# Selection masks in a sparse-attention block: expanded by matmuls with a 0/1 matrix, or read back from a stored copy with repeated rows

## The reference, cut to what matters

```
importance = einsum('bgsn,nm->bgsm', sum(p_cmp, axis=2), overlap)    # (B, G, S, 32)
sel_score  = where(forced & valid, 1e4, where(valid, importance, -1e4))
_, sel_idx = top_k(sel_score, 16)             # per query and group: 16 of 32 blocks of 64 keys
mask       = key_pos <= t                     # inside the chosen blocks
p          = masked_softmax(q @ K_chosen, mask);  out = p @ V_chosen
```

## Time and profile before

| what | value |
|---|---|
| times of the runs shown | 6959.97, 7552.63 (the median), 7947.71 us |
| profiled execution | 6946.9 us, its span 6945.3 us |
| cores in it | even 6864.7 to 6872.9 us, odd 6942.8 to 6945.4 us |
| PE busy | 6812.9 us (98%) |
| PE on the chain that ended last | 93% |
| DVE, ACT busy | 2238.7 us (32%), 1169.3 us (17%) |
| stage B of core 1 | from about 1394 to 2600 us, attention until about 2500 us |

### The profile page before, as it was taken

How to read it: one execution, slowest core, us unless ns; L and a number is a source line. 1 busy time by engine, 2 the same in 40 slices (tenths; PEclk the granted TensorE clock), 3 DMA queues, 4 the chain that set the end, 5 groups by cost and what they waited for, 6 DMA issues and landing times.

```text
span 6945.3 us, 98178 instructions; the slowest of 8 cores (6864.7 to 6945.4 us)
## 1 busy us (share of the span) xinstructions
PE 6812.9 (98%) x37468; PEld 3534.2 (51%) x37468; DVE 2238.7 (32%) x4038; ACT 1169.3 (17%) x2168; POOL 452.0 (7%) x727
## 2 busy tenths in 40 slices
PE   7999999989999999999999999999999999999997
PEld 4644454445555544466654444444444444444665
DVE  5418889544444513324430111111111111111134
ACT  4001110234444410013320000000000000000221
POOL 0000000000000000011100000000000000000110
PEclk9999999999999999999999999999999999999999
DMA  9645655778764355678854456775676766644798
GB/s 253 156 91 96 111 104 106 163 124 146 140 131 101 73 127 121 118 204 290 296 116 79 97 117 135 122 120 121 154 168 116 122 124 154 141 78 81 232 322 310
DMA packets 312533, 1017.19 MB, mean 146 GB/s; under 512 B 27360, under 2 KB 113248, under 8 KB 286720
## 3 DMA queue, kind: packets, MB, share of 16 engines
q0 software_dynamic: 160176, 707.98, 51.8%
q1 hardware_dynamic: 149440, 298.72, 13.1%
q10 hardware_dynamic: 2448, 4.13, 0.2%
HBM read 1381.75 MB, written 202.70 MB: 228 GB/s over the span
## 4 chain that ended last, share of the span: by engine, by line
PE 93%; DMA 3%; DVE 1%; issue 1%; SPq 1%; ACT 1%; DVEq 0%; ACTq 0%; POOLq 0%
PE bank L1403 54%; PE bank L352 28%; PE bank L1435 6%; PE bank L1143 2%; PE bank L1118 2%; DMA xr<-xc_t 1%; SPq L131 1%; DMA p_conv<-cstg 1%; PE bank L769 0%; DMA p_q<-sgb 0%; PE bank L1215 0%; DMA wslot<-w_dn_b 0%; DMA out<-yr 0%; DVE yr L1724 0%; DMA p_kv<-sgb 0%
## 5 line engine op out<-in xcount | busy, mean ns | idle before, releaser
L1403 PE MATMUL bank<-merged,wslot 128*128 128x496 bf16 (+2 forms) x11264 | 2119.4, 351 | 1.7 <-DVE merged L1444 1.7
L352 PE MATMUL bank<-uT,wslot 128*128 128x496 bf16 (+1 forms) x8768 | 1900.2, 375 | 0.0
L1403 PE MATMUL bank<-actq,wslot 128*128 128x496 bf16 (+2 forms) x9216 | 1718.2, 349 | 5.4 <-DMA wslot<-w_dn_b 4.1
L1403 PEld LDWEIGHTS bank<-merged,wslot 128*128 128x128 bf16 x11264 | 1102.1, 98 | 1018.3 <-issue 2.7
L352 PEld LDWEIGHTS bank<-uT,wslot 128*128 128x128 bf16 x8768 | 856.7, 98 | 952.5 <-issue 6.3
L1403 PEld LDWEIGHTS bank<-actq,wslot 128*128 128x128 bf16 x9216 | 901.3, 98 | 821.7 <-issue 8.0
L1595 DVE SCALAR_TENSOR_TENSOR rlE<-bank,acc 128x496 f32<-128x496 f32 (+2 forms) x262 | 173.5, 662 | 1489.0 <-PE bank L1403 1488.6
L1601 ACT ACTIVATE actq<-rlE 128x496 bf16<-128x496 f32 (+2 forms) x262 | 159.0, 607 | 2804.1 <-DVE rlE L1595 2804.1
L665 DVE SCALAR_TENSOR_TENSOR yb<-glu,cps,yb 128x992 f32<-128x992 f32 x480 | 600.0, 1250 | 43.2 <-DVE yb L665 1.8
L1121 ACT ACTIVATE emt<-bank 128x512 bf16<-128x512 f32 (+1 forms) x736 | 349.3, 529 | 367.3 <-PE bank L1118 268.0
L1650 DVE TENSOR_TENSOR ost<-bank,part 128x496 f32<-128x496 f32 x128 | 86.3, 674 | 770.3 <-PE bank L1403 770.3
(11 more groups left out here) (180 smaller groups left out, 3075.5 us busy)
## 6 DMA issues: line engine op xcount, KB each, us to landing
wslot<-w_in_t POOLq DMA_DIRECT2D x150, 1024.0 KB, 10.2
wslot<-w_up_t POOLq DMA_DIRECT2D x122, 1024.0 KB, 8.9
wslot<-w_out_b POOLq DMA_DIRECT2D x96, 1024.0 KB, 6.8
...
```

The source lines that it names most:

```text
L352: fns = [lambda kc=kc, bk=bk: nc.tensor.matmul(bk[:, 0:n], wt[:, kc * 128:(kc + 1) * 128], rhs[:, kc, lo:lo + n], start=(kc == 0), stop=(k ...
L1403: fns = [lambda kc=kc: nc.tensor.matmul(bk[:, 0:n], wt[:, kc * 128:(kc + 1) * 128], rhs[:, kc, lo:lo + n], start=(kc == 0), stop=(kc == KC ...
```

## The change

`expand` by matmuls and casts goes. The turned choice `selT` is stored in DRAM (`p_sel`, one 32 x 512 slice for each step), and the mask tiles are read back from it: for a group of 4 key tiles two loads, one into partitions 0 to 63 and one into 64 to 127, each repeating a row of 512 queries over 64 partitions. The steps of the choice move: `sel_transpose` from `wj0` + 11 to `wj0` + 5, the loads come at `wj0` + 6 and `wj0` + 7, the diagonal cuts at `sj0` - 4 to `sj0` - 1, `load_q` and `load_kv` from `wj0` + 8 to `wj0` + 12. `emats` and its clearing by DVE, and that of `selT`, go on the odd cores. Lines after the top of the file move by one or two: L1206 is L1204 afterwards, L1143 is L1141, L1118 is L1116, L1157 is L1155.

```diff
--- before.py
+++ after.py
@@ -186,6 +186,7 @@
     p_ga = dscr("p_ga", [32, 128, TMAX], BF16)
     p_gb = dscr("p_gb", [32, 128, TMAX], BF16)
     p_attn = dscr("p_attn", [16, 128, TMAX], BF16)
+    p_sel = dscr("p_sel", [8, 32, 512], BF16)
     p_conv = dscr("p_conv", [16, 128, TMAX], BF16)
     p_x1 = dscr("p_x1", [128, KC * TMAX])
     w_out_b = dscr("w_out_b", [32, 128, D], BF16)
@@ -931,14 +932,14 @@
             obf = Tile("obf", [128, 4, 512], BF16, Rw.end)
             ostg = Tile("ostg", [128, 2, 512], BF16, obf.end)
             imp = Tile("imp", [128, 4, 32], F32, ostg.end)
-            KE = 128 if h else 32
-            selT = Tile("selT", [KE, 512], BF16, imp.end)
+            selT = Tile("selT", [32, 512], BF16, imp.end)
             selm = Tile("selm", [128, 4, 32], BF16, selT.end)
             tk = Tile("tk", [128, 2, 32], F32, selm.end)
             mx = Tile("mx", [128, 16], F32, tk.end)
             sm = Tile("sm", [128, 12], F32, mx.end)
-            emats = Tile("emats", [KE, 2048], BF16, sm.end)
+            emats = Tile("emats", [32, 1024], BF16, sm.end)
             assert emats.end <= eb["lo"]
+            pselB = [Buf() for _ in range(8)]
             goff = gatesT_off - base
             selvs = Tile("selvs", [128, NT * 32], F32, goff + 2048)
             selbs = Tile("selbs", [128, NT * 32], F32, goff + 3072)
@@ -986,13 +987,10 @@
             VT = ((False, 0, 8), (False, 8, 4), (True, 0, 8), (True, 8, 8)) if h else ((False, 0, 8), (False, 8, 0), (True, 0, 8), (True, 8, 0))
             load_kv(0, ("vs",))
             if h:
-                K.op(dve, lambda: nc.vector.memset(emats[:], 0.0), w=[ematB])
-                K.op(dve, lambda: nc.vector.memset(selT[:], 0.0), w=[selTB])
-            K.dma(sp, emats[0:32, :], emat[:, :], w=[ematB])
-            if h:
                 K.dma(sp, selvs[:], selv[:, :], w=[selvB])
                 K.dma(sp, selbs[:], selb[:, :], w=[selbB])
             else:
+                K.dma(sp, emats[:], emat[:, 0:1024], w=[ematB])
                 K.dma(sp, tmk[:], tmsk[:, :, :], w=[tmkB])
                 K.dma(sp, tsl[:], tsel[:, :, :], w=[tslB])
                 K.dma(sp, wpd[:], wpad[:, :], w=[wpdB])
@@ -1206,18 +1204,19 @@
                 fns = [lambda t=t: nc.tensor.transpose(out=pst[0:32, t * 128:(t + 1) * 128], in_=selm[:, t, :], identity=idb[:])
                        for t in range(4)]
                 K.group(pe, fns, r=[selmB, constB], w=[bb])
-                K.op(act, lambda: nc.scalar.copy(out=selT[0:32, :], in_=pst[0:32, 0:512]), r=[bb], w=[selTB])
-
-            def expand(s, jt):
-                bk, bb = ring_bank("aux")
-                lo = max(0, jt * 128 - (1024 + (s % 2) * 512))
-                diag = jt * 128 >= 1024 + (s % 2) * 512
-                K.op(pe, lambda: nc.tensor.matmul(bk[:, lo:512], emats[:, jt * 128:(jt + 1) * 128], selT[:, lo:512], start=True, stop=True),
-                     r=[selTB, ematB], w=[bb])
-                K.op(act, lambda: nc.scalar.copy(out=msk[:, jt, lo:512], in_=bk[:, lo:512]), r=[bb], w=[mskB[jt]])
-                if diag:
-                    K.op(dve, lambda: nc.vector.tensor_tensor(out=msk[:, jt, lo:lo + 128], in0=msk[:, jt, lo:lo + 128], in1=tri[:, 0, :],
-                                                              op=ALU.mult), r=[triB], w=[mskB[jt]])
+                K.op(act, lambda: nc.scalar.copy(out=selT[:], in_=pst[0:32, 0:512]), r=[bb], w=[selTB])
+                K.dma(sp, p_sel[s], selT[:], r=[selTB], w=[pselB[s]])
+
+            def expand(s, j0, j1):
+                src = p_sel[s].rearrange("(j k) q -> k j q", k=2)
+                for k in range(2):
+                    K.dma(sp, msk[k * 64:k * 64 + 64, j0:j1, :], src[k, j0:j1, :].unsqueeze(0).to_broadcast([64, j1 - j0, 512]),
+                          r=[pselB[s]], w=mskB[j0:j1])
+
+            def diagonal(s, jt):
+                lo = jt * 128 - (1024 + (s % 2) * 512)
+                K.op(dve, lambda: nc.vector.tensor_tensor(out=msk[:, jt, lo:lo + 128], in0=msk[:, jt, lo:lo + 128], in1=tri[:, 0, :],
+                                                          op=ALU.mult), r=[triB], w=[mskB[jt]])
 
             def finish(s, hh):
                 g, qg = s // 2, s % 2
@@ -1276,13 +1275,15 @@
                 if h:
                     for t in range(4):
                         at(wj0 + t, lambda s=s, t=t: topk(s, t))
-                    at(wj0 + 11, lambda s=s: sel_transpose(s))
-                    for jt in range(njt):
-                        at(wj0 + 13 + jt, lambda s=s, jt=jt: expand(s, jt))
+                    at(wj0 + 5, lambda s=s: sel_transpose(s))
+                    for i in range(njt // 4):
+                        at(wj0 + 6 + i // 2, lambda s=s, i=i: expand(s, 4 * i, 4 * i + 4))
+                    for jt in range(njt - 4, njt):
+                        at(sj0 + jt - njt, lambda s=s, jt=jt: diagonal(s, jt))
                 if s + 1 < 8:
-                    at(wj0 + 8, lambda s=s: load_q(s + 1))
+                    at(wj0 + 12, lambda s=s: load_q(s + 1))
                 if qg == 1 and g + 1 < 4:
-                    at(wj0 + 8, lambda g=g: load_kv(g + 1, ("vs", "vw", "ks", "kw")))
+                    at(wj0 + 12, lambda g=g: load_kv(g + 1, ("vs", "vw", "ks", "kw")))
                     for i, (sel, b0, n) in enumerate(VT):
                         at(sj0 + 10 + 4 * i, lambda g=g, sel=sel, b0=b0, n=n: vtrans(g + 1, sel, b0, n))
```

## The result

The changed kernel is slower by a ratio of 1.0165 (95% interval 1.0121 to 1.0208): two runs took 7072.7 and 7075.3 us, and two of the kernel before 6958.8 and 6960.0. The median of all four runs is 7128.98 us (7072.69 to 7224.23); that of the kernel before, 7256.3. The profiled execution took 7075.3 us.

What follows compares the result with a forecast made beforehand. PE's stream on the odd cores was taken to set the time. The terms -21.0 - 1.9 - 11.8 + 41.6 - 2.3 + 18.4 + 48 gave +71, so 6947 + 71 = 7018 us, range 6952 to 7125 us.

Steps and rivals of the forecast that it cites:

- Matmuls that go: PE on the odd cores: 112 expansion matmuls vanish, -21.0 us, and waits for ACT's casts, -1.9 us.
- Start of B: Start of stage B: without the clearings PE's 18 us idle time shortens, -11.8 us.
- The turning: At the earlier transposes PE waits for VectorE's last selm in all eight steps, +41.6 us.
- Clock: Behind the eight waits at the transposes PE's work runs at clock 0.50, 2.3 us lost each, +18.4 us.
- absorbed waits: Step 0: an existing PE wait of the next head for the same late VectorE disappears, -2.3 us.
- Masks: Diagonal cuts: mask loads chained through SP's pairs land late; 100 us of PE waits, halved for draining queues, +48 us.
- The draining: Mask loads: once PE stands, POOL issues less traffic and queues drain, so 100 us of waits was halved to 50.
- The bounds, 0 and 109: Limits of the mask-wait term: 0 at the best landings, 109 us with no draining and four clock tolls.
- A: Rival at the diagonal cuts: masks late in every step, 252 us instead of 48, 7222 us; chance 0.23.

Runs made afterwards that it cites:

- e1: The changed kernel with the two halves of the mask tiles tracked separately, so neither load waits for the other; odd cores 6974.6 us.
- e2: The kernel before with only the transposes of the choice moved from wj0 + 11 to wj0 + 5, expansions still by matmuls; odd cores 6999.9 us.
- e9: The changed kernel with each key tile's mask read by one 128 KB load over all 128 partitions instead of paired half loads; odd cores 7236.1 us.

## Why the prediction was wrong, point by point

The range, 6952 to 7125 us, holds the 7073 and 7075 us of the runs compared and misses the median of 7129.0 by 4 us. The sum said +71 us. The slowest core of the runs is 115 us above before, the mean of the odd cores 109; 12 us more of the distance from 7018 to 7074 come from the starting point, since the profiled execution (6946.9 us) lay below all other runs of before. Taken by the steps:

1. **Matmuls that go, -22.9: right.** e1 has the turning of e2 and no mask waits, and its lag grows by 18 us less (31 against 49) although a wait of 8.8 us came in, so they are worth 18 to 27 us.
2. **Start of B, -11.8: right.** -9 us on the mean of the four (-6 to -16). Both details came as worked out: the second head's backs start at 1413.9 us (forecast 1416.3), and VectorE waits for the store behind `dsp1` until 1410.8 (forecast 1412.9).
3. **The turning, wait +41.6: right (43.3). Clock +18.4: right in kind and a little high,** an estimated 14 to 16 us by e2. The 2.3 us of absorbed waits were 5.5. Together 57.7 us were forecast and 49 measured.
4. **Masks, +48: right in mechanism, half in size,** and **this is the step that failed.** e1 shows the chain through the pairs, at 87 us with its clock. The waits of the steps 0 to 7 were 23.0, 21.0, 24.4, 12.6, 3.5, 3.9, 0 and 1.9 us, 90 in all; I had 11, 46, 11, 28, 0, 2, 0, 2, 100 in all, and then halved them, "once PE stands, the queues drain". The draining is seen in step 1, where loads issued at 1640 to 1646 us, while PE stands, land after 4.4 to 5.2 us and those issued before them after 13 to 17; but it shortens the chain in the steps 1 and 3 alone. The steps 0 and 2, for which one row had stood, have longer chains than worked out, and no halving of their waits is seen. From the issue of the store to the last landing the steps took 55, 52, 56, 44, 34, 35, 30 and 34 us, where the chain was worked out as 46, 81, 46, 63, 31, 37, 31 and 37. The first mask load of a step lands after 3.6 to 5.9 us, the slowest after 9 to 19 (step 0, then step 1, min/median/max):

```profile
DMA to landing us min/median/max: 4.9/10.5/19.4
DMA to landing us min/median/max: 4.4/9.2/17.0
```

   PE's wait is the chain less 30 to 32 us in all seven steps that wait. I had 35: the 31.8 us of the earlier trace rows were read with the expansions between the transposes and the cut, and those go with the change (12 or 16 of them at 0.21 us, an estimated 2.5 to 3.4 us a step). The bounds, 0 and 109, held.
5. **Stage EF is no term and no rival.** The wait of 15 us there is real and goes with the neighbour's traffic, and the profile had the distance of 77 us and 14.4 us of VectorE's waits for `out<-yr` just under PE's cover. It accounts for 13 us against the profiled execution, but for none of the 109 us between the runs, to which the other runs of before give 12 to 16 us of their own. It belongs to the starting point, not to the change.

Attention as a whole came to 118 us where the steps gave 83, and the start of B to 9 where they gave 12: these two make up the 38 us by which the 109 miss the sum of 71.

Of the rivals A (masks late in every step) had the right place; its 252 us were too much, and at 87 us the term stayed under A's threshold of 116. The rule of the Trainium skill (DMA: Bandwidth & Descriptors, section Rules for kernel authors) that one transfer over 128 partitions is better than two over disjoint halves gets no fair test here. Two halves without a wait between them left no PE wait for masks (e1), and the one load over 128 partitions cost some 260 us more (e9); but that load moved on 0.13 of the DMA engines, and a load over 128 partitions that uses them all was not run. The fixed cost of about 2 us that the prediction takes from the Trainium skill (same page, section Anatomy of one DMA) stands there for transfers that POOL issues, and these are SP's: in the changed kernel the stores of the choice landed after 1.5 to 8.1 us, and no mask load in under 3.6. Another page of the Trainium skill (HBM Reference, section Specifications) gives two cores of a pair about 716 GB/s together; the 630 to 658 measured while both are busy stay below it.

Open: by what rule the pair's bandwidth is shared, and so why the loss in stage EF rises again between 145 and 200 us of distance and is largest near 0.
